# Reordering the groups of experts of a two-level mixture-of-experts stage on one core

## What is computed

```python
def hierarchical_moe(h, w_rg, b_rg, w_re, b_re, w_gate, w_up, w_down):
    ...
    expert_id = gidx * EXPERTS_PER_GROUP + eidx          # top group of 4, then top 2 of its 4 experts
    combine = jnp.sum(jax.nn.one_hot(expert_id, N_EXPERTS) * ew[..., None], axis=1)
    y = jnp.zeros_like(t)
    for e in range(N_EXPERTS):                            # 16 experts, 1024 -> 512 -> 1024
        he = jax.nn.silu(t @ w_gate[e]) * (t @ w_up[e])
        y = y + combine[:, e:e + 1] * (he @ w_down[e])
x = x + hierarchical_moe(...);  return rms_norm_2(x, g_final)
```

## Time and profile before

| | |
|---|---|
| median of 3 runs | 2130.97 us (2130.12 to 2132.14) |
| the profiled execution | 2127.3 us, of which 2125.5 us from first to last instruction (the span) |
| mean granted TensorE clock | 0.983 of full speed |
| busy in the span: TensorE, VectorE, ScalarE, POOL | 2037.7, 1265.5, 984.0, 138.9 us |
| HBM read / written | 307.12 MB / 33.03 MB |
| weight transfers of the expert stage into the RAW buffers (gate, up, down), 512 KB each | 58, 61 and 62 |

### The profile page before, as it was taken

The page is one execution under the profiler, slowest core; times in us unless marked ns, Lnnn a source line. Parts: engine busy times, 40 slices in busy tenths (PEclk is TensorE's granted clock), DMA queues, the critical chain, the costliest instruction groups (busy, mean ns, idle before and its releaser), DMA issues.

```text
span 2125.5 us, 27884 instructions
## 1 busy us (share of the span) xinstructions
PE 2037.7 (96%) x10483; PEld 1596.6 (75%) x10483; DVE 1265.5 (60%) x2204; ACT 984.0 (46%) x1630; POOL 138.9 (7%) x239
## 2 busy tenths in 40 slices
PE   8999999999999999979999999999899999889997
PEld 7877778888888877758888888878688887446542
DVE  5575766575846356656756856737644466347552
ACT  4445545445534355544554454533653253146551
POOL 0000020000001000001000002102000001101110
PEclk9999999999999999989999999999999999989999
DMA  6235234642632324313425353443435335999894
GB/s 212 70 104 176 92 119 142 205 149 74 204 109 80 123 96 138 110 35 125 152 73 193 104 198 98 140 126 116 128 95 168 107 128 220 376 406 405 283 308 171
DMA packets 193999, 337.92 MB, mean 159 GB/s; under 512 B 16039, under 2 KB 103351, under 8 KB 193857
## 3 DMA queue, kind: packets, MB, share of 16 engines
q1 hardware_dynamic: 190096, 327.09, 45.6%
q0 software_dynamic: 3760, 8.96, 1.8%
HBM read 307.12 MB, written 33.03 MB: 160 GB/s over the span
## 4 chain that ended last, share of the span: by engine, by line
PE 79%; DVE 7%; DMA 5%; ACT 3%; POOL 2%; issue 2%; SPq 2%; DVEq 0%; ACTq 0%; POOLq 0%
PE ps L183 74%; PE ps L186 5%; POOL SM L218 1%; SPq L223 1%; DVE WL L198 1%; ACT ST L194 1%; POOL SM L215 1%; ACT WH L194 1%; DMA ONDP<-qkd 1%; DMA RAW<-in_w_down_dram 1%; DMA XG<-hd,IDX 1%; DVE X L208 1%; DMA ed<-ST 1%; DMA NQ<-qqd 0%; DMA qkd<-ST 0%
## 5 line engine op out<-in xcount | busy, mean ns | idle before, releaser
L198 DVE TENSOR_TENSOR WL<-RAW,WH 128x1024 fp32r<-128x1024 f32 x395 | 477.0, 1222 | 272.4 <-ACT WH L194 268.9
L194 ACT ACTIVATE WH<-RAW 128x1024 fp32r<-128x1024 f32 x395 | 412.1, 1056 | 326.8 <-PE ps L183 193.7
L183 PE MATMUL ps<-XH,WH 128*128 128x512 f32 (+1 forms) x880 | 323.9, 368 | 3.7 <-DVE WL L198 3.7
L183 PE MATMUL ps<-XL,WH 128*128 128x512 f32 (+1 forms) x880 | 321.0, 365 | 0.0
L183 PE MATMUL ps<-XH,WL 128*128 128x512 f32 (+1 forms) x880 | 320.6, 364 | 0.0
L183 PE MATMUL ps<-WH,XH 128*128 128x512 f32 (+1 forms) x736 | 297.1, 404 | 2.4 <-ACT ST L194 2.4
L183 PE MATMUL ps<-WH,HR 128*128 128x512 f32 x928 | 289.2, 390 | 0.0
L183 PE MATMUL ps<-WH,XL 128*128 128x512 f32 (+1 forms) x736 | 285.0, 387 | 0.0
L183 PE MATMUL ps<-WL,XH 128*128 128x512 f32 (+1 forms) x736 | 284.3, 386 | 0.0
L183 PEld LDWEIGHTS ps<-WH,HR 128*128 128x128 f32 x928 | 174.2, 188 | 36.0
L183 PEld LDWEIGHTS ps<-XH,WH 128*128 128x128 f32 x880 | 168.1, 191 | 30.3 <-DVE WL L198 4.6
(11 more groups left out here) (368 smaller groups left out, 2863.5 us busy)
## 6 DMA issues: line engine op xcount, KB each, us to landing
RAW<-in_ffn_w_dram SPq DMA_DIRECT2D x164, 512.0 KB, 4.6
RAW<-in_w_down_dram SPq DMA_DIRECT2D x62, 512.0 KB, 12.9
RAW<-in_w_up_dram SPq DMA_DIRECT2D x61, 512.0 KB, 11.6
RAW<-in_w_gate_dram SPq DMA_DIRECT2D x58, 512.0 KB, 12.1
RAW<-in_w_in_dram SPq DMA_DIRECT2D x30, 512.0 KB, 4.5
RAW<-in_ev_w_in_dram SPq DMA_DIRECT2D x20, 512.0 KB, 4.5
RAW<-in_ple_w_gate_dram SPq DMA_DIRECT2D x16, 512.0 KB, 4.2
RAW<-in_od_w_in_dram SPq DMA_DIRECT2D x32, 256.0 KB, 3.4
```

The lines of the kernel that those rows point to most:

```text
L183: return self.go(ns).matmul(o, lhsT=l, rhs=x, start=st, stop=sp)
L194: return self.go(0.83 * n + 55.0 + (130.0 if bias is not None else 0.0) + (100.0 if acc is not None else 0.0)).activation(o, i, f, scale=s ...
L198: return self.go(1.04 * n + 68.0).tensor_tensor(o, a, b, op)
```

## The change

`GROUPS` gets another order. Slot 0 stays first; slot 2 (three experts) follows it in place of slot 1; then come the seven single experts, the two with second slots early among them; slot 1 (four experts) becomes the last, which is the slot that is added on the chip. As slot 2 is now scattered and slot 1 is not, the lists in PUT are made for slot 2's three experts (32, 32, 64 rows) instead of slot 1's four. PUT shrinks from 18 to 17 columns.

```diff
-    route[:, 584:588] = np.where(p[:, None] // 32 == np.arange(4), 0, 1000)
+    route[:, 584:587] = np.where(np.minimum(p[:, None] // 32, 2) == np.arange(3), 0, 1000)
...
-    PUT = zone("PUT", 69, [128, 18], U32)
+    PUT = zone("PUT", 69, [128, 17], U32)
...
-    GROUPS = ((0,), (1,), (7,), (6,), (8, 10), (5,), (9, 11), (4,), (3,), (2,))
+    GROUPS = ((0,), (2,), (8, 10), (7,), (9, 11), (6,), (5,), (4,), (3,), (1,))
...
-            v.tt(PUT[:, 14:18], ROUTE[:, 584:588], pf[:, 1:2].broadcast_to([128, 4]), ALU.add, 4).then_inc(*v.sig("dve_vec"))
+            v.tt(PUT[:, 14:17], ROUTE[:, 584:587], pf[:, 2:3].broadcast_to([128, 3]), ALU.add, 3).then_inc(*v.sig("dve_vec"))
...
-                lists = [PUT[:, i:i + 1]] if i not in SHARED else [PUT[:, 12 + p:13 + p] for p, _, _ in SHARED[i]]
+                lists = [PUT[:, i:i + 1]] if i not in SHARED else [PUT[:, m:m + 1] for m in {0: (12, 13), 2: (14, 15, 16)}[i]]
```

## The result

The changed kernel is slower: 2142.15 us median (2139.27 to 2146.03) against 2130.55 us for the kernel before on the same chip, ratio 1.0058, 95% interval 1.0038 to 1.0078. A second session gave 1.0075 (1.0048 to 1.0102). The profiled execution's span is 2137.4 us, 11.9 more than before.

What follows compares the result with a forecast made beforehand. The expert stage was taken as short of DMA bandwidth early, paced by TensorE later, with DMA idle at the end. T0 2052.35 + 53.9 gave end of spread 2106.25, -8.2 us, hence 2122.8 us; eight in ten 2114 to 2137.

Steps and rivals of the forecast that it cites:

- Three-expert slot second: Slot 2's fan and fold after slot 0: no tile waits, some 18 us lead; the four-expert slot's 18.7 us loss goes.
- I count its 5.0 us as gone: Loss behind the first double slot (8, 10), 2.8 + 2.2 us, expected to vanish because fold(2) needs no splitting.
- I keep the whole 7.0 us: Loss behind the second double slot (9, 11), laid to ScalarE's list order, expected to stay; possible range 0 to 15.8 us.
- T0: Mark where the fan of the last slot begins; forecast at 2052.35 us, against 2053.2 in the kernel before.
- the small edits at nothing: Three PUT lists instead of four, one scatter of some 8 us fewer on POOL, PUT's narrower last write: no cost.
- the losses stay: Rival: 15.8 us beside the four-expert slot come from ScalarE and VectorE list order; sum +0.6, 2131.6 us; chance 0.20.
- the tail is worse: Rival: the last 28 tiles share the queue with X loads and sums, spread at low clock; +5.5, 2136.5 us; chance 0.17.
- Starves too: Rival: the three-expert slot also waits for tiles, price 18.7 us back; +10.5, 2141.5 us; chance 0.03.
- T0 past 2060, with ScalarE or VectorE as releaser: Sign of being wrong: the last slot's fan begins after 2060 us, its waits released by ScalarE or VectorE.
- The tail: From the last slot's fan to end of spread: TensorE starves some 14 us, ending at T0 + 53.9, against + 61.3 before.
- T0 + 41.5: Landing of the last of 28 weight tiles in the tail: first lands 4.6 us after issue, 27 follow at 1.34 us.
- The return of X: Four X loads at the end, behind the last weights, land at T0 + 47; spread does not wait, 1 to 2 us in hand.

Runs made afterwards that it cites:

- e8_pool_only: Changed kernel with two gathers moved back behind sums on POOL's list alone, other engines' lists untouched; ratio 1.0003 to the kernel before.
- e9_tail_double: From e4_time, the second double slot (9, 11) moved to last but one; ratio 0.9948 to the kernel before.
- e11_no_sum3: From e8_pool_only, the sum of slot 3 left out (result incomplete); last fold step began at T0 + 46.9 instead of T0 + 49.2, tail stayed 58.3 us.
- e10_change_again: The changed kernel as it is, measured again beside the others on one chip; ratio 1.0075 to the kernel before.
- e4_time: Changed kernel with the build-time planner told that a gather or sum lands 7 us after issue, all lists laid out anew; ratio 0.9979 to the kernel before.
- e12_time_again: e4_time measured once more with more rounds; ratio 0.9978 to the kernel before.

## Why the prediction was wrong

It said 2122.8 us, faster by 8.2 (2114 to 2137); it came to 2142.15. By its own steps:

**Three-expert slot second: right.** No wait for a tile, clock 1.00, 32.5 us for a fan that I put at 31.9. The lead held.

**Double slots: right in the work, wrong in what hangs on them.** "I count its 5.0 us as gone": fan(7), fold(8, 10) show no loss. "I keep the whole 7.0 us": with POOL's list mended, the losses to T0 are 208.0 - 200.65 = 7.35 us. The size is partly luck, for the wait is another for the most part. I kept 3.47 us on the evacuation that frees the fold's banks; in e8_pool_only TensorE waits 1.36 us for that at 1988.66 and 3.13 us for a copy of VectorE (EG) at 1986.60, and the clock is 0.76 in the 12 us behind it. Both are gone in e9_tail_double, where that slot stands last but one.

**The step that failed** is the sentence that costed the small edits at nothing: "Scatters and gathers share POOL's list; the first scatters had over 30 us to spare." The spare was there in TensorE's time, but a list that waits in order spends it on whatever stands in front. The earlier trace rows show sums 8 to 10 us apart, and in the trace of before the third sum of slot 1 was already some 36 us late (1963.76, where 1918.69 and a turn of 9 us give 1928). I read late sums as harmless because they had been harmless, and did not ask which buffers they hold and what would now want them. Price: 220.0 - 208.0 = 12.0 us in that profile. The rivals did not hold it: "the losses stay" and "the tail is worse" were the nearest, and both had another mechanism. "Starves too" gave 2141.5, which lies near the measured time by chance: the three-expert slot did not starve. One of the signs of being wrong did come true, "T0 past 2060, with ScalarE or VectorE as releaser": T0 is 2068.9, and VectorE releases the two long waits.

The spans add up: the forecast's -8.2, +12.35 from fan to T0, +3.5 ahead of the first fan, +3.2 in the tail, +1.0 before the stage and in the final norm make the measured +11.9.

**The stretch ahead of the first fan was not costed.** It took 33.5 us instead of 30.0. One microsecond is the turn of slot 10's rows, which now falls inside fold(0). The rest goes with the clock there. The same window in both kernels, after first:

```profile
1838.00:1842.00 4.00, 3.22 (x12) 0.93 (x12) 0.69 (x1) 0.00 (x0) 0.19 (x1) 0.70 1.02 409
1842.00:1846.00 4.00, 4.00 (x22) 1.73 (x20) 0.00 (x0) 0.60 (x1) 0.74 (x1) 0.88 1.03 410
```

```profile
1838.00:1842.00 4.00, 4.00 (x20) 1.29 (x18) 0.00 (x0) 0.00 (x0) 0.00 (x0) 1.00 1.03 413
```

The low clock follows on gaps that both kernels have. Over all profiles this stretch took 29.7 to 32.7 us where a single expert's slot comes third and 30.9 to 36.0 where the double slot does, so some of the 3.5 us belongs to the change and some to the run; how much stays open.

**The tail: mechanism right, size off.** TensorE starved from the seventh fan step on, each step of the last fold waited, the X loads were no obstacle. The end of spread came at T0 + 57.1 and not + 53.9. The term that was too small is "T0 + 41.5" for the last landing: it was T0 + 48.0 (2116.91). I let the first of the 28 tiles meet an empty queue and land after 4.6 us, the time of an earlier stage's weights; the same page of before has medians of 11.6 to 12.9 us for the expert weights. The queue was running at 387 GB/s before T0, with tiles still in flight: the seventh step waited until T0 + 13.5 where the landing line gave about + 10. And the sum of slot 3 takes bandwidth: 2.3 us by e11_no_sum3, one execution. Against that, the last step ran at full clock (1.92 us) and the spread in 7.19, 3.3 us less than I had put. That last step was luck of the profiled execution. Of the eleven profiles with slot 1 last it took 1.92 or 1.93 us in three and 3.25 to 3.64 us in eight; the same code took 1.92 in the kernel after and 3.25 in e10_change_again, 3.64 in e4_time and 1.92 in e12_time_again. So 3.6 us was the usual case, and it was right to have it in the sum, with the range for the other. By the Trainium skill, "TensorE: Matmul & The Clock Gate", HAM oscillation, every burst starts at the low clock when short bursts stand between longer waits for DMA. The trace agrees in part: in the kernel after, the third of the four steps of the last fold, behind the longest wait (5.56 us), took 3.64 us, and the others 1.92.

**The return of X: right in the outcome.** That the loads "cannot overtake the weights" was more than I could take from the order in which transfers are taken up, which does not say when they land. In e11_no_sum3, with the loads issued 10.9 us sooner, the last weights were not late.

**"Losses stay" as a measure of the swap.** Even with the sums on time the change in its own order is level with before (1.0003), not 0.4% ahead: -0.5 at T0 and -2.9 in the tail, with +3.6 before the first fan. Starvation moved from one end to the other for the most part. It pays only with the lists rearranged (0.9978) or with a double slot in front of the starved one (0.9948).

## What to carry to other kernels

When a change reorders work, follow each buffer to the step that frees it, and that step to its place in its engine's list: a transfer that is late in an in-order list is free only as long as nobody wants its buffer. A starved stage at the end needs other work beside it: a group with much compute per byte right before it paid here (e9_tail_double, 0.9948 against 0.9978 in the same session). When buffers are handed out by a plan, check that the next user gets the one that is free first. If a static schedule comes from a model, look first at which entries of one engine's list waited while the next one was ready.

## What the runs showed of the hardware

A sum to memory costs the weights time while it runs: in e8_pool_only the rate fell from 401 to 277 GB/s at a DMA share of 1.09, in the kernel after from 410 to 264 GB/s. Leaving out one sum of 128 rows (512 KB) brought the last step of the fold forward by 2.3 us, where a weight tile of 512 KB takes 1.34 us; against the other profiles it is 1.1 to 3.9 us, so that it costs more than its bytes is likely but not shown.

Bursts of 16 matmul records between waits of 1.4 to 5.6 us took 1.92 us in some cases and 3.64 in others, at the same step of the same fold; the last one took 1.93 in e8_pool_only and 3.64 in e11_no_sum3, and the gain of 2.3 us was lost that way.
